# Two edits to a two-layer diffusion step: the latents' expert choice in two halves of the token list with the third weight loaded behind the gathers, and the last expert's rows added on the chip

## The reference, cut to what matters

```python
def _expert_choice(h, router_w, w1, w3, w2):          # once for latents, once for context
    C = max(1, EC_CAPACITY * N // N_EXPERTS)          # 64 of 512 latents, 16 of 128 context tokens
    aff = jax.nn.softmax((xs @ router_w).astype(jnp.float32), axis=-1)
    gate, idx = lax.top_k(aff.T, C)                   # each expert takes its C best tokens
    xe = xs[idx]
    he = jax.nn.silu(jnp.einsum('ecd,edf->ecf', xe, w1)) * jnp.einsum('ecd,edf->ecf', xe, w3)
    ye = jnp.einsum('ecf,efd->ecd', he, w2) * gate[..., None].astype(h.dtype)
    out = jnp.zeros_like(xs).at[idx.reshape(-1)].add(ye.reshape(-1, D))
    ...
# layer:  x = x + gate2 * _expert_choice(h, ...)      then the next layer's RMSNorm, or the final one
```

## Time and profile before

| what | value |
|---|---|
| three runs of the kernel before | 2001.81, 2003.74, 2004.12 us; median 2003.74 us |
| the profiled execution's own time | 1998.4 us |
| its span | 1996.6 us, 27163 instructions |
| PE busy | 1839.6 us (92%) |
| DVE busy | 1541.4 us (77%) |
| ACT busy | 1156.2 us (58%) |
| POOL busy | 313.6 us (16%) |
| chain that ended last, by engine | PE 87%, DVE 6%, DMA 3%, ACT 2%, issue 2%, POOL 1% |
| chain, by line | experts' products (L1086) 53%, input projection (L790) 10%, output projection (L967) 5% |

### The profile page before, as it was taken

How to read it: one execution, slowest core, us unless ns; L and a number is a source line. 1 busy time by engine, 2 the same in 40 slices (tenths; PEclk the granted TensorE clock), 3 DMA queues, 4 the chain that set the end, 5 groups by cost and what they waited for, 6 DMA issues and landing times.

```text
span 1996.6 us, 27163 instructions
## 1 busy us (share of the span) xinstructions
PE 1839.6 (92%) x9522; PEld 1300.0 (65%) x9522; DVE 1541.4 (77%) x2280; ACT 1156.2 (58%) x1540; POOL 313.6 (16%) x142
## 2 busy tenths in 40 slices
PE   4999999959999999999969999996999999999993
PEld 2776777836666666666657786784566666666662
DVE  4543647589999999999756364667899999999993
ACT  2410356238777777777542115624677777787772
POOL 0100021010222122222012003111022122122210
PEclk9999999969999999999979999996999999999996
DMA  9568201289999999999852721026899999999973
GB/s 344 180 229 306 85 1 43 95 307 356 379 387 382 371 387 372 382 388 380 294 158 88 277 77 69 12 106 248 314 372 383 382 381 379 376 380 378 388 294 129
DMA packets 86219, 542.02 MB, mean 271 GB/s; under 512 B 6880, under 2 KB 9698, under 8 KB 61572
## 3 DMA queue, kind: packets, MB, share of 16 engines
q1 hardware_dynamic: 75556, 504.10, 65.0%
q0 software_dynamic: 10592, 36.97, 6.9%
HBM read 517.19 MB, written 23.86 MB: 271 GB/s over the span
## 4 chain that ended last, share of the span: by engine, by line
PE 87%; DVE 6%; DMA 3%; ACT 2%; issue 2%; POOL 1%; SPq 0%; DVEq 0%; ACTq 0%; POOLq 0%
PE bank L1086 53%; PE bank L790 10%; PE bank L967 5%; PE bank L683 2%; PE bank L915 2%; PE bank L1096 1%; PE bank L1103 1%; PE bank L826 1%; PE bank L900 1%; PE bank L930 1%; PE bank L1005 1%; PE bank L988 1%; PE bank L1038 1%; DMA ring<-in_ada_w 1%; DMA arena_z<-xn_dram,icur 1%
## 5 line engine op out<-in xcount | busy, mean ns | idle before, releaser
L1366 ACT ACTIVATE arena_h_r<-ring 128x1024 fp32r<-128x1024 f32 x480 | 504.5, 1061 | 160.3 <-PE bank L1086 157.5
L1879 DVE TENSOR_TENSOR ring_r<-ring,arena_h_r 128x1024 fp32r<-128x1024 f32 x470 | 556.9, 1218 | 22.9 <-ACT arena_h_r L1366 16.1
L1086 PE MATMUL bank<-arena_h_r,arena_u_r 128*80 128x512 f32 x1280 | 371.2, 396 | 0.1
L1879 DVE TENSOR_TENSOR ring_r<-ring,arena_u_r 128x1024 fp32r<-128x1024 f32 x282 | 333.9, 1221 | 13.3 <-ACT arena_u_r L1366 6.7
L1366 ACT ACTIVATE arena_u_r<-ring 128x1024 fp32r<-128x1024 f32 x288 | 301.0, 1059 | 61.2 <-PE bank L1086 61.2
L1086 PE MATMUL bank<-ring_r,arena_u_r 128*80 128x512 f32 x1024 | 317.3, 391 | 0.0
L1086 PEld LDWEIGHTS bank<-arena_h_r,arena_u_r 128*80 128x80 f32 x1280 | 187.3, 150 | 97.0 <-DVE arena_u_r L1899 3.2
L1086 PE MATMUL bank<-arena_u_r 128*80 128x512 f32 x768 | 216.9, 391 | 0.0
L1086 PEld LDWEIGHTS bank<-ring_r,arena_u_r 128*80 128x80 f32 x1024 | 151.6, 148 | 84.6 <-issue 0.4
L644 POOL DMA_INDIRECT x_res<-arena_z,iscat x32 | 90.7, 2835 | 643.5 <-DVE arena_z L1925 643.5
L638 POOL DMA_INDIRECT arena_z<-xn_dram,icur x32 | 142.3, 4446 | 313.1 <-issue 274.1
(11 more groups left out here) (253 smaller groups left out, 2636.3 us busy)
## 6 DMA issues: line engine op xcount, KB each, us to landing
ring<-in_exp_w SPq DMA_DIRECT2D x192, 2048.0 KB, 9.9
ring<-in_ada_w SPq DMA_DIRECT2D x24, 2048.0 KB, 8.8
ring<-in_w_in SPq DMA_DIRECT2D x8, 2048.0 KB, 19.6
ring<-in_w_out SPq DMA_DIRECT2D x2, 4096.0 KB, 13.5
x_res<-arena_z POOLq DMA_DIRECT2D x10, 512.0 KB, 3.3
xn_dram<-arena_u POOLq DMA_DIRECT2D x10, 512.0 KB, 3.0
arena_z<-x_res SPq DMA_DIRECT2D x10, 512.0 KB, 5.8
arena_z<-x_res POOLq DMA_DIRECT2D x5, 512.0 KB, 3.8
```

Source lines behind the costliest of these rows:

```text
L1086: mm = pe.matmul(bank[out + n][0:CAP, :], xs[:, c, :], w[:, n * 512:(n + 1) * 512], start=(c == 0 and part == 0), stop=(c == KC - 1 and pa ...
L1366: act.activation(high[c], slot[s][:, c, :], ACT.Copy).then_inc(high_ready, 1)
L1879: v.tensor_tensor(slot_r[s][:, c, :], slot[s][:, c, :], high[c], ALU.subtract).then_inc(low_ready, 1)
```

## The change: what it does

1. **Two halves.** Experts' affinities for latents 0 to 255 go to partitions 0 to 15 and those for 256 to 511 to partitions 32 to 47, and `top_round` works on 48 partitions x 256. Each half gives a sorted list of 64. PE turns the first list upright and the second upright, and then multiplies the second by a reversed identity (`turn64`), so that place k of the first stands beside place 63 - k of the second. The larger of each such pair is one of the 64 best (`lists_merged`). The context rounds come after it.
2. **Order around it.** `norm2_T(2)`, `router(1)` and `router(2)` move between the halves of projection 3, `h2(2)` ahead of `gated1(3)`; three instead of four chunks of the last half stand ahead of the turning of the affinities; seven fillers stand ahead of `norm2_T(4)` and one ahead of `router(4)`. The four copies that write `g2e` and `s2e` move from behind the first gather's issue to ahead of `logit_max`.
3. **Third weight.** Both of its halves wait for both gathers.
4. **The last rows.** Of the last expert, DVE makes a table `places` (80 partitions x 640 tokens, 1 where the row belongs), PE multiplies it with the expert's rows, and DVE adds the product to the residual tile, which SP has loaded early (`rows_staged`, once the scatter of the expert before is done). In layer 0 the scatter to DRAM stays, since the residual is read from there again, but nobody near waits for it; in layer 1 it is gone. The six fillers ahead of layer 1's projections are gone. The order of squares, means and normalisation over the tiles is new in layer 1 and at the end.

```diff
@@ sync @@
+            def rows_staged(l):
+                sp.wait_ge(scattered, ((l - 1) * EXPERTS + EXPERTS - 1) * 16)
+                for t in range(NT):
+                    sp.dma_start(staged[t], x_res[t * P:(t + 1) * P]).then_inc(x_in[t], 16)
...
+                if l:
+                    sp.wait_ge(x_sum, (l - 1) * NT + NT)
                 sp.dma_start(win, i["window"].rearrange("(t p) n -> p t n", p=P)).then_inc(prm_in, 16)
...
                     w_in_load(l, 1)
+                    rows_staged(l)
...
-                    sp.wait_ge(scattered, l * EXPERTS * 16)
-                    for t in range(NT):
-                        sp.dma_start(zt[:, t, 0:D], x_res[t * P:(t + 1) * P]).then_inc(x_in[t], 16)
...
-                        if s == 2 and before is None and h:
+                        if s == 2 and before is None:
                             for u in range(2):
                                 sp.wait_ge(xe_in[u], l * (PAIRS * 16) + 16)
@@ tensor @@
+                    if l:
+                        pe.wait_ge(x_sum, (l - 1) * NT + (3, 4, 4, NT, NT)[t])
...
-                w_out_half(4, 0)
+                w_out_half(4, 0, 0, 6)
                 norm2_T(3)
-                router(2)
+                w_out_half(4, 0, 6, KC)
                 router(3)
-                w_out_half(4, 1, 0, KC // 2)
+                w_out_half(4, 1, 0, 3)
                 pe.wait_ge(aff_done, l * 2 + 1)
...
+                pe.wait_ge(x1_done, l * NT + 4)
+                keep_clock(7, 1)
                 norm2_T(4)
-                pe.wait_ge(x1_done, l * NT + 4)
+                keep_clock(1, 1)
                 router(4)
+                pe.wait_ge(top_done, l * 3 + 1)
...
                 pe.wait_ge(ye_done, l * EXPERTS + EXPERTS)
+                for t in range(NT):
+                    if t == NT - 1:
+                        pe.wait_ge(x_sum, l * NT + 1)
+                    for x in range(2):
+                        mm = pe.matmul(bank[SUM_BANK[t] + x][:, :], places[:, t * P:(t + 1) * P],
+                                       ye_last[:, x * 512:(x + 1) * 512], start=True, stop=True)
+                    mm.then_inc(sum_mm, 1)
@@ vector @@
+            def summed(l, t):
+                v.wait_ge(x_in[t], (l + 1) * 16 + 16)
+                v.wait_ge(sum_mm, l * NT + t + 1)
+                for x in range(2):
+                    cols = slice(x * 512, (x + 1) * 512)
+                    ins = v.tensor_tensor(zt[:, t, cols], bank[SUM_BANK[t] + x][:, :], staged[t][:, cols], ALU.add)
+                ins.then_inc(x_sum, 1)
...
-                for c in range(3):
+                for c in range(4):
                     first_rest(c)
-                for dst, n in ((g2e, 3), (s2e, 2)):
-                    ...
-                first_rest(3)
```

More of the change, by code:

```diff
@@ L753, in _ @@
                 pe.wait_ge(mod_out, steps_to(ADA * l + 2))
-                for _ in range(6):
-                    pe.matmul(bank[7][:, 0:KC * CT], ident, cs[:, :, :].rearrange("p k s -> p (k s)"), start=True, stop=True)
+                if l == 0:
+                    for _ in range(6):
+                        pe.matmul(bank[7][:, 0:KC * CT], ident, cs[:, :, :].rearrange("p k s -> p (k s)"), start=True, stop=True)
                 for n, (kind, t, _) in enumerate(proj):
@@ L1042, in _ @@
                     w_out_half(n, 0)
+                    if n == 3:
+                        norm2_T(2)
+                        router(1)
                     w_out_half(n, 1)
+                    if n == 3:
+                        router(2)
                     if n == 1:
@@ L1057, in _ @@
                 pe.wait_ge(aff_done, l * 2 + 1)
                 for t in range(4):
-                    mm = pe.transpose(bank[7][0:EXPERTS, t * P:(t + 1) * P], aff[:, t, :], ident)
+                    at = t // 2 * 32
+                    mm = pe.matmul(bank[7][at:at + EXPERTS, (t % 2) * P:(t % 2 + 1) * P], aff[:, t, :], ident,
+                                   start=True, stop=True)
                 mm.then_inc(affT_mm, 1)
-                w_out_half(4, 1, KC // 2, KC)
+                w_out_half(4, 1, 3, KC)
@@ new lines, in _ @@
+                pe.wait_ge(top_done, l * 3 + 2)
+                pe.matmul(bank[1][0:CAP_L, 2 * EXPERTS:4 * EXPERTS], turn64, lower, start=True, stop=True).then_inc(top_mm, 1)
+                pe.wait_ge(top_done, l * 3 + 3)
+                for n, x in enumerate((topf, topv)):
+                    mm = pe.matmul(bank[4][CAP_L:CAP, n * EXPERTS:(n + 1) * EXPERTS], x[0:EXPERTS, CAP_L:CAP],
+                                   ident[0:EXPERTS, 0:EXPERTS], start=True, stop=True)
+                mm.then_inc(top_mm, 1)
@@ L1470, in phase @@
                 def phase(n):
+                    if l and n == 0:
+                        v.wait_ge(rows_free, l * EXPERTS + 2)
                     v.wait_ge(f_mm, l * 2 + n + 1)
@@ L1495, in taps, with mean1 @@
                     v.wait_ge(f3_out, l * NT + t + 1)
-                def normed(t):
+                def mean1(t):
                     c = slice(t, t + 1)
@@ L1555, in _ @@
                     v.wait_ge(mod_out, steps_to(ADA * l + 2))
-                    w_in_rest(0)
+                    summed(l - 1, 0)
+                    summed(l - 1, 1)
+                    mean1(0)
+                    w_in_rest(0, 0, 2)
                     normed(0)
+                    mean1(1)
+                    summed(l - 1, 2)
+                    w_in_rest(0, 2, 4)
+                    h1(0)
                     normed(1)
-                    for t in range(NT):
+                    h1_rest(0)
+                    summed(l - 1, 3)
+                    w_in_rest(0, 4, 6)
+                    h1(1)
+                    w_in_rest(0, 6, KC)
+                    mean1(2)
+                    h1_rest(1)
+                    normed(2)
+                    for t in range(2, NT):
+                        if t + 2 < NT:
+                            summed(l - 1, t + 2)
                         h1(t)
-                        if t < NT - 2:
-                            normed(t + 2)
+                        if t + 1 < NT:
+                            mean1(t + 1)
                         h1_rest(t)
+                        if t + 1 < NT:
+                            normed(t + 1)
                 def conv(m):
@@ L2017, in tables @@
     c["sel"] = s
+    c["places"] = np.tile(np.arange(TOK), (CAP, 1))
+    c["turn64"] = np.eye(64)[::-1]
     return {n: a.astype(np.float32) for n, a in c.items()}
```

218 lines of the change are left out of this document (151 added, 67 removed).

## The result

| | before | changed |
|---|---|---|
| median of 5 runs | 2003.74 us (1999.19 to 2007.24) | 1993.53 us (1990.09 to 1997.97) |
| ratio | 1 | 0.9948, 95% interval 0.993 to 0.9967 |
| span of the profiled execution | 1996.6 us | 1994.3 us |
| PE, DVE, ACT, POOL busy | 92, 77, 58, 16% | 94, 78, 58, 15% |

The change is faster, by 10.2 us and not by 17.8, and the median lies 1.5 us above the range. The direction was right; more than half of the gain in the expert choice is missing.

The account below looks back on a forecast made before the run. PE's chain was taken as the bound, with gains only where it leaves PE: 5.5 + 7.0 + 0.5 + 4.8 = 17.8 us, so 2003.74 - 17.8 = 1985.9 us. Range 1979 to 1992.

Parts of the forecast that it names:

- the gain in the expert choice: From output projection to first product: 5.5 us gained in layer 0 and 7.0 in layer 1.
- Rounds and hops: VectorE's list rounds at 1.36 us instead of 2.16, plus added hops: indices 6.2 us earlier in layer 0, 7.7 in layer 1.
- the clock behind layer 1's router passes: Layer 1's 12 output-projection matmuls, split up, should run at the high clock: 1.5 us gained.
- Part 2, the gather's issue: First gather: GpSimd ends 5.9 us after the indices instead of 5.3, beside four subtractions; 0.7 us lost per layer.
- Part 3 and the landing: Third weight behind both gathers: costs nothing (bound 0.3 us); a gather lands 3.9 us after GpSimd's end.
- I cost the removal at nothing: Taking the third weight's first half out of the queue ahead of the gather changes nothing; bound 0.3 us.
- covered: Third weight: a half lands 9.9 us after issue, both within 15, needed some 35 us after the gather; no wait.
- the case of gains hidden by the weights' stream: Rival: weights' stream bounds from the gather on, earlier start waited away in the loop; only 4 to 6 us remain; 2%.
- From the landing to the first product nothing changes: Between gather landing and first expert product: transposes, 3.49 us of filler and modulation stay as they were.
- Part 4a, the boundary: Between the layers: first projection 5 us earlier, given back by a period of 8.1 us against 6.37; gain 0.5.
- Part 4b, the end: After the last expert: last scaling ends at 1988.3 instead of 1993.13; gain 4.8 us, bounds 0 and 6.
- 1.2 GHz: Rival: the ten products run at the low clock, a tile every 3.5 us instead of 1.9; gain 10 us; 10%.

Follow-up runs that it names:

- copies_back: The changed kernel with the four copies that write g2e and s2e put back between VectorE's subtractions; 1993.50 us, ratio 0.9949 to the kernel before.
- early: The changed kernel with 3.5 MB of the first expert's weights loaded earlier, while the queue was idle; 1981.78 us, ratio 0.9896 to the kernel before.
- third_alone: The kernel before with only the third weight's edit (both halves wait for both gathers); 2005.40 us, ratio 1.0016 to the kernel before.
- gate_first: The changed kernel plus 3.5 MB of early weight loads, with the copy of gateT's context rows moved ahead of icur's copies; 1985.02 us, ratio 0.9911 to the kernel before.
- boundary: The changed kernel with only the order of VectorE and ScalarE work at layer 1's start changed; 1986.28 us, ratio 0.9907 to the kernel before.
- sums_alone: The kernel before with only the last expert's part: staged rows, ten products, sums on chip, new order; 1996.66 us, ratio 0.9964 to the kernel before.

## Why the prediction was wrong, step by step

**Rounds and hops: right in kind, slightly too hopeful.** A round on half the list takes 406.25 - 404.88 = 1.37 us (1.36 predicted), by VectorE's timeline:

```profile
404.00 0.84 DVE L1974 COPY spectrum<-bank 16x256 f32<-16x256 f32 x2 [0.78 <-PE bank L1090]
404.88 0.42 DVE L1925 MAX8 topv<-spectrum 48x8 f32<-48x256 f32 x1
...
406.25 0.42 DVE L1925 MAX8 topv<-spectrum 48x8 f32<-48x256 f32 x1
```

The stretch to `icur` is 23.3 us instead of 22.6. The start of the lists did not come 0.6 earlier but stands at 68.7 from W, 68.4 before. So 4.6 instead of 6.2 in layer 0, 6.6 instead of 7.7 in layer 1. Of the latter 1.5 were for the clock behind layer 1's router passes. This pair of profiles bears it out, but the fall is bound neither to that layer nor to the old order: in layer 0, the first nine matmuls of the last half took 2.14 us in the changed kernel's profile and 3.18 in that of copies_back, where the granted clock was 0.65 from 400.00 to 403.40.

**Part 2, the gather's issue: wrong sign.** I took 0.7 us as lost; 3.0 were gained at GpSimd. I had read the duration off the kind and number of VectorE's operations, and it hangs on a quarter of a microsecond in their start. The Trainium skill (SBUF — State Buffer, Who interferes with whom) blames copies and infers that `tensor_tensor` leaves the writing of descriptors alone; here copies made no difference in either kernel, and subtractions alone stood beside 1.4 us as well as beside 4.6. The measurement decides. By what mechanism the start decides was not tried.

**Part 3 and the landing: the step that failed.** The prediction put the landing 3.9 us behind GpSimd's end ("I cost the removal at nothing"), called the weights "covered", and gave the case of gains hidden by the weights' stream 2 in 100. In the trace of before the second weight landed 1.1 us after the gather was issued, and the first half of the third 1.3 us before the gather's landing. An issue 4.6 us earlier had to meet it, and the weight moved the other way besides: it waits for tile 4's store, which took 8.1 us instead of 4.1, as the view of that store shows (from issue to landing),

```profile
L651 POOL DMA_DIRECT2D xn_dram<-arena_u x1: 531/531/531, 415.0 to 415.0; - x1
...
DMA to landing us min/median/max: 8.1/8.1/8.1
```

most likely because the first weight, let go at 407.6 by the end of the output projection, was still on its way: it went out 11.2 us ahead of this store before and 7.4 now, and its second half landed at 421.9. In early, where half of it had gone out before, the same store took 3.5 us. early shows the cause of the long gather by taking it away: 4.45 us. That price is 2.6 us in layer 0 and 2.7 in layer 1 against 8.26 and 7.94, on top of 3.0 gained at GpSimd that could not show. Even the 3.9 us behind GpSimd's end held some waiting: with the third weight's half gone (third_alone) it was 3.1, and 3.1 in gate_first with a free queue.

**"From the landing to the first product nothing changes"** held (5.0 us, 4.9 before). Behind it, though, the second expert's first weight came late: product to loop 30.7 and 35.1 us where it was 30.0 and 30.1. I had looked at the third weight's own use, 35 us off, and not at what is queued behind it. The term was put at nothing; third_alone puts it at 1.9 us per layer on the kernel before.

Term by term for the choice: layer 0 gained 4.6 at the indices and 3.0 at GpSimd, lost 5.6 from GpSimd's end to the landing, 0.1 to the product and 0.7 behind it, which leaves 1.2 where 5.5 were predicted. In layer 1 the same terms are 6.6, 3.0, -5.7, -0.1 and -5.0: a loss of 1.3 by the table, where a gain of 7.0 was predicted.

**Part 4a, the boundary: hit.** The period is 7.85 us (8.1 predicted), by PE's timeline, where L1180 are the ten products and L759 the transposes:

```profile
1007.29 8.85 PE L1180 MATMUL bank<-arena_u 80*128 80x512 f32 x20 [1.50 <-DVE arena_u L2061]
1016.97 1.13 PE L759 MATMUL bank<-cst,arena_z 128*128 128x128 f32 x8 [0.83 <-DVE arena_z L1538]
1023.48 1.94 PE L759 MATMUL bank<-cst,arena_z 128*128 128x128 f32 x8 [5.38 <-DVE arena_z L1538]
...
1032.12 1.16 PE L759 MATMUL bank<-cst,arena_z 128*128 128x128 f32 x8 [0.38 <-DVE arena_z L1585]
...
1039.97 1.16 PE L759 MATMUL bank<-cst,arena_z 128*128 128x128 f32 x8 [1.21 <-DVE arena_z L1585]
...
1047.82 1.16 PE L759 MATMUL bank<-cst,arena_z 128*128 128x128 f32 x8 [1.22 <-DVE arena_z L1585]
```

From the last expert's result (1007.24) to projection 3 (1048.98) it is 41.7 us; before, 1003.61 to 1046.06 = 42.5. Gained 0.7, with 0.5 predicted; and boundary shows that the order alone gave the rest away.

**Part 4b, the end: right, slightly small.** From the last expert's result to the last scaling's end:

```profile
1971.47 1.40 DVE L2061 SCALAR_TENSOR_TENSOR arena_u<-bank,gateT,gate 80x512 f32<-80x512 f32 x2 [7.51 <-PE bank L1131]
...
1988.70 2.48 DVE L2110 SCALAR_TENSOR_TENSOR arena_z<-arena_z,sroot,arena_h 128x1024 f32<-128x1024 f32 x2
```

18.3 us against 1993.13 - 1969.57 = 23.6: 5.3 gained, 4.8 predicted. The ten products took 8.85 us at PEclk 1.00, not 1.2 GHz. Another 1.0 us in each layer is the last expert's own last product (12.8 us, 13.7 before); such a microsecond comes and goes between the profiles (74.3 and 75.1 for the old end), and I credit it to neither part.

**The sum.** Predicted were 5.5 + 7.0 + 0.5 + 4.8 = 17.8. The profile gives 1.2 - 1.3 at the loops, 0.7 between the layers, 5.3 at the end and 0.9 + 1.3 in the last experts' products and the tail, 8.1 in all; the timings of the halves give 4.2 and 7.2 by their ratios. The two terms of the choice failed, those of the sums held: in kind and in size by the profile, and within a wide interval by the time.

## What to carry to other kernels

When a step on the path is made earlier, look up what its transfer will share the queue with at the new time. Here a gather that was issued a few microseconds behind 4 MB took some 11 us, and 4.3 to 4.5 with those bytes out of the way; a landing taken from a queue that was just running dry did not carry over. When the chain shows no transfer, that says only that it was covered up to now; count the bytes from the last idle stretch of the queue to the point where each is used. If they don't fit, move bytes into the idle stretch first; here the choice's half of the change was worth some 4 us without that, and the whole change with 3.5 MB moved gave 10 to 12 more.

## What the runs showed of the hardware that was not expected

- GpSimd's issue of a layer's first 80-row gather took 1.4 to 1.5 us at 0.60 to 0.70 us behind the start of VectorE's row of subtractions, and 4.4 to 4.6 at 0.83 to 0.96, in both layers of all 17 traces. No gather fell in between, and by what mechanism the start decides was not tried.
- A 2 MB half issued ahead of a gather did not lengthen that gather where 4 MB were already on their way (11.06 us against 10.87; the gather landed 7.6 us ahead of that half), and cost it 3 us where the queue was nearly free (101.6 against 98.5 from W; it landed 1.3 us behind the half).
- The granted clock fell behind the router passes in some layers and stayed at 1.00 in others, with the same code: in the five traces with the old expert choice, 12 output-projection matmuls took 2.8 to 2.9 us, 4.3 to 4.4 or 4.9 to 5.0, the last at a granted clock of 0.55 (sums_alone, layer 0).
- The start of the output projection of layer 0 varied from 329.5 to 336.8 us over the profiles, in code that no edit touched; a single span cannot be read to better than that here.
